# Unread columns left out in block two, the rotated keys' tile holds both weight parts, modulation chunks regrouped, square-root table loads moved, output in four pieces

## What is computed

```
# block one, two layers, both token streams
shift, scale, gate = split(silu(c) @ w_ada[l] + b_ada[l])        # modulation
h = rms(x, norm_w[l]) * (1 + scale) + shift
qa, ka, va, qb, kb, vb, cq, ckv, kpe, z = split(h @ w_in[l])     # kpe: 64 columns, rotated keys of the third head group
x = x + gate * (concat(attention a, b, c) * silu(z)) @ w_out[l]

# block two, 16 meta tokens ahead of the 256 latent ones
hn = rms_norm(h, norm_mix_g)
u, gb_in, gc_in, v_in, ga_lin, gbr_lin = split(hn @ w_in_2)
y_a = pool(u) @ pool_w      # group i: mean over the last 2, 4, 8 or 16 positions, minus the token itself
y_b = (gb_in * causal_conv3(gc_in * v_in)) @ conv_out_w
h = h + (sigmoid(ga) * y_a + sigmoid(gbr) * y_b) @ w_o
h = h + (silu(gate) * up) @ w_down                               # of rms_norm(h) @ w_gate_up
return rms_norm(h, norm_final_g)[:, 16:]                         # the 16 meta positions are dropped
```

## Time and profile before

| | |
|---|---|
| median of 3 runs | 3471.76 us (3467.4 to 3475.43) |
| the profiled execution's own time | 3463.28 us |
| its span, first to last instruction | 3462.0 us |
| PE busy | 3311.9 us, 96% of the span |
| DVE, ACT busy | 1650.5 us (48%), 1359.4 us (39%) |
| granted PE clock, mean | 0.982 of full speed |
| read from HBM | 550.07 MB |

### The profile page before, as it was taken

How to read it: one execution, slowest core, us unless ns; L and a number is a source line. 1 busy time by engine, 2 the same in 40 slices (tenths; PEclk the granted TensorE clock), 3 DMA queues, 4 the chain that set the end, 5 groups by cost and what they waited for, 6 DMA issues and landing times.

```text
span 3462.0 us, 52180 instructions
## 1 busy us (share of the span) xinstructions
PE 3311.9 (96%) x21982; PEld 2870.4 (83%) x21982; DVE 1650.5 (48%) x2678; ACT 1359.4 (39%) x2179; POOL 172.5 (5%) x252
## 2 busy tenths in 40 slices
PE   6799999988999989999799999999999999999998
PEld 1488888863458888887459999999999999999998
DVE  0422233374563363355575675555555645545444
ACT  1422232344442263333454443344444444444343
POOL 2000000001001101000101000000000000000000
PEclk9999999998999999999899999999999999999999
DMA  9533222226744254443436455555555555555554
GB/s 344 187 122 122 91 93 96 84 74 239 251 174 151 92 193 142 140 134 108 156 119 200 151 182 177 182 178 189 186 186 188 165 186 187 189 186 186 189 185 138
DMA packets 154314, 566.06 MB, mean 164 GB/s; under 512 B 17472, under 2 KB 19648, under 8 KB 152928
## 3 DMA queue, kind: packets, MB, share of 16 engines
q1 hardware_dynamic: 147648, 529.52, 45.7%
q0 software_dynamic: 6432, 33.20, 2.7%
HBM read 550.07 MB, written 12.58 MB: 163 GB/s over the span
## 4 chain that ended last, share of the span: by engine, by line
PE 88%; DMA 5%; DVE 3%; ACT 2%; issue 1%; POOL 0%; SPq 0%; DVEq 0%; ACTq 0%; POOLq 0%
PE ps L695 20%; PE ps L696 20%; PE ps L697 20%; PE ps L688 7%; PE ps L690 7%; PE ps L689 7%; DMA sb_raw<-in_stream 5%; PE ps L614 2%; PE ps L816 1%; PE ps L802 1%; PE ps L779 1%; PE ps L795 1%; PE ps L770 1%; DVE sb_wlo L1236 1%; PE ps L727 1%
## 5 line engine op out<-in xcount | busy, mean ns | idle before, releaser
L1236 DVE TENSOR_TENSOR sb_wlo<-sb_raw,sb_whi 128x1024 fp32r<-128x1024 f32 (+1 forms) x818 | 996.8, 1219 | 1355.0 <-ACT sb_whi L891 1354.5
L891 ACT ACTIVATE sb_whi<-sb_raw 128x1024 fp32r<-128x1024 f32 (+1 forms) x818 | 859.4, 1051 | 1141.9 <-PE ps L697 912.3
L695 PE MATMUL ps<-sb_hn_hi,sb_whi 128*128 128x256 f32 (+1 forms) x2944 | 832.3, 283 | 4.1 <-DVE sb_hn_lo L1301 4.1
L696 PE MATMUL ps<-sb_hn_lo,sb_whi 128*128 128x256 f32 (+1 forms) x2944 | 832.7, 283 | 0.0
L697 PE MATMUL ps<-sb_hn_hi,sb_wlo 128*128 128x256 f32 (+1 forms) x2944 | 831.4, 282 | 0.0
L695 PEld LDWEIGHTS ps<-sb_hn_hi,sb_whi 128*128 128x128 f32 x2944 | 556.2, 189 | 4.7 <-DVE sb_hn_lo L1301 4.5
L696 PEld LDWEIGHTS ps<-sb_hn_lo,sb_whi 128*128 128x128 f32 x2944 | 555.8, 189 | 0.0
L697 PEld LDWEIGHTS ps<-sb_hn_hi,sb_wlo 128*128 128x128 f32 x2944 | 555.7, 189 | 0.0
L690 PE MATMUL ps<-sb_whi,sb_lo 128*128 128x512 f32 (+1 forms) x968 | 374.3, 387 | 0.0
L695 PE MATMUL ps<-sb_hi,sb_whi 128*128 128x512 f32 (+1 forms) x1056 | 359.9, 341 | 14.8 <-DVE sb_lo L1284 14.8
L696 PE MATMUL ps<-sb_lo,sb_whi 128*128 128x512 f32 (+1 forms) x1056 | 357.7, 339 | 0.0
(11 more groups left out here) (259 smaller groups left out, 3959.3 us busy)
## 6 DMA issues: line engine op xcount, KB each, us to landing
sb_raw<-in_stream SPq DMA_DIRECT2D x992, 512.0 KB, 3.4
sb_raw<-in_stream SPq DMA_DIRECT2D x18, 384.0 KB, 3.1
sb_T<-in_x POOLq DMA_DIRECT2D x1, 4096.0 KB, 16.0
z_scratch<-sb_scr POOLq DMA_DIRECT2D x16, 256.0 KB, 2.5
sb_zb<-z_scratch POOLq DMA_DIRECT2D x16, 256.0 KB, 3.4
sb_bias<-in_bias POOLq DMA_DIRECT2D x4, 1024.0 KB, 10.1
x_scratch<-sb_T POOLq DMA_DIRECT2D x1, 4096.0 KB, 11.5
sb_T<-in_x POOLq DMA_DIRECT2D x2, 1536.0 KB, 7.5
```

The source lines that it names most:

```text
L695: PE.matmul(o, whi[:, s, w], xh, start=k == 0, stop=False)
L696: PE.matmul(o, whi[:, s, w], xl, start=False, stop=False)
L891: AC.activation(whi[:, s, 0:width], raw[:, r, 0:width], ACT.Copy).then_inc(*hi.up((g.id, c)))
L1236: VE.tensor_tensor(wlo[:, s, 0:width], raw[:, r, 0:width], whi[:, s, 0:width].bitcast(F32), ALU.subtract).then_inc(*lo.up((g.id, c)))
```

## The change

It has five parts.

1. In block two, `u`, `gc` and `v` are made only for the columns that are read later: the last 256 plus the window's length (258, 260, 264, 272) for `u`, the last 258 for `gc` and `v`. The token operand now starts at column 272 - n of its row. The pooling sums on DVE and the copies out of PSUM are narrowed alike.
2. For `kpe`, DVE writes the low part over the second 64 columns of `whi`, so that one stationary tile holds both parts. PE runs two products per inner tile in place of three, and the four transposes become four float32 products with a constant 128x64 matrix, "fold" (two unit matrices one above the other), which adds the halves.
3. `ADA_PACE` of layer 0 goes from 3, 3, 2, 0 chunks in four slots to 4, 2, 2, 0.
4. The four "sqrt_table" steps go from behind the last squares to the first chunk of the third of the four groups of `wout`, `wo` and `down`.
5. At the end DVE multiplies tile by tile with the norm's weight while `down` still runs, into a new tile `scaled`; when the norm is there, four multiplications of 1024 columns follow, and SP sends each piece (512 KB) by a transfer of its own.

```diff
--- before.py
+++ after.py
...
-ADA_PACE = ([8, 0] + [3, 3, 2, 0] * 11, [8, 0] + [2, 2, 2, 2, 0, 0] * 3)
+ADA_PACE = ([8, 0] + [4, 2, 2, 0] * 11, [8, 0] + [2, 2, 2, 2, 0, 0] * 3)
...
-    ("ident", P), ("band", 5 * P), ("cols", GRID_W), ("cos", 2 * HD), ("sin", 2 * HD), ("mean", 1), ("sum4", 2),
+    ("ident", P), ("fold", HD), ("band", 5 * P), ("cols", GRID_W), ("cos", 2 * HD), ("sin", 2 * HD), ("mean", 1), ("sum4", 2),
...
     for g in range(4):
-        mix.append(Group("u", None, g, DT, 512, span(512 * g), N2, "hn", 4, "w_in_2", "hn_mix" if g == 0 else None))
+        mix.append(Group("u", None, g, DT, 512, span(512 * g), L + WINDOWS[g], "hn", 4, "w_in_2", "hn_mix" if g == 0 else None))
     for j in range(4):
-        mix.append(Group("gc", None, j, DT, 512, span(2 * D + 512 * j), N2, "hn", 1, "w_in_2"))
+        mix.append(Group("gc", None, j, DT, 512, span(2 * D + 512 * j), L + 2, "hn", 1, "w_in_2"))
...
-        mix.append(Group("v", None, j, DT, 512, span(3 * D + 512 * j), N2, "hn", 1, "w_in_2"))
+        mix.append(Group("v", None, j, DT, 512, span(3 * D + 512 * j), L + 2, "hn", 1, "w_in_2"))
...
                 self.add("chunk", g, c)
+                if g.kind in ("wout", "wo", "down") and g.index == 2 and c == 0:
+                    self.add("sqrt_table")
...
         pl.flush()
-        pl.add("sqrt_table")
...
     pl.flush()
-    pl.add("sqrt_table")
...
     pl.flush()
-    pl.add("sqrt_table")
...
-    x_out, out_out = sig("x_out", 16), sig("out_out", 16)
+    x_out = sig("x_out", 16)
+    out_out = [sig(f"out_out{j}", 16) for j in range(4)]
...
+    SCALED = sb("scaled", [P, DT, L], F32, hn_at + 4 * N2 * 4)
...
         if g.x in ("hn", "latent"):
-            a = META if g.x == "latent" else 0
+            a = 0 if g.kind == "ffn" else N2 - g.n
             return NH[:, k, a:a + g.n], NL[:, k, a:a + g.n]
...
-        SP.wait_ge(*v_ev.at("final"))
-        SP.dma_start(d["out"], RES[:, :, META:]).then_inc(*out_out.up("out"))
-        SP.wait_ge(*out_out.at("out"))
+        for j in range(4):
+            SP.wait_ge(*v_ev.at("final", j))
+            SP.dma_start(d["out"][:, 4 * j:4 * j + 4, :], SCALED[:, 4 * j:4 * j + 4, :]).then_inc(*out_out[j].up("out"))
+        for j in range(4):
+            SP.wait_ge(*out_out[j].at("out"))
...
@@ -692,6 +695,10 @@
                     for t in range(g.width // P):
                         o = PS[:, g.base + t, 0:g.n]
                         w = slice(w0 + t * P, w0 + t * P + P)
+                        if g.kind == "kpe":
+                            PE.matmul(o, whi[:, s, w], xh, start=k == 0, stop=False)
+                            mm = PE.matmul(o, whi[:, s, w], xl, start=False, stop=k == g.kt - 1)
+                            continue
                         PE.matmul(o, whi[:, s, w], xh, start=k == 0, stop=False)
                         PE.matmul(o, whi[:, s, w], xl, start=False, stop=False)
                         mm = PE.matmul(o, wlo[:, s, w], xh, start=False, stop=k == g.kt - 1)
...
                     for t in range(4):
-                        mm = PE.transpose(PS[:, g.base, t * P:(t + 1) * P], SC[:, 7, t * P:(t + 1) * P], ident)
+                        mm = PE.matmul(PS[:, g.base, t * P:t * P + HD], SC[:, 7, t * P:(t + 1) * P], C("fold"), start=True,
+                                       stop=True)
                     mm.then_inc(*e_ev.up(("kpt", l)))
...
-                AC.activation(T2[:, 4 * (p % 2), 16:16 + N2], PS[:, g.base + p, 0:N2], ACT.Copy).then_inc(
+                AC.activation(T2[:, 4 * (p % 2), 16 + N2 - g.n:16 + N2], PS[:, g.base + p, 0:g.n], ACT.Copy).then_inc(
...
-                    ins = AC.activation(CV[:, m, 0:N2], PS[:, g.base + m, 0:N2], ACT.Copy)
+                    ins = AC.activation(CV[:, m, META - 2:N2], PS[:, g.base + m, 0:g.n], ACT.Copy)
...
+            if g.kind == "kpe":
+                v = whi[:, s, 0:width].rearrange("p (a b) -> p a b", b=P)[:, :, HD:P]
+                w_ = raw[:, r, 0:width].rearrange("p (a b) -> p a b", b=P)[:, :, HD:P]
+                VE.tensor_tensor(v, w_, v.bitcast(F32), ALU.subtract).then_inc(*lo.up((g.id, c)))
+                return
...
+        def scaled_out(k):
+            VE.tensor_scalar(SCALED[:, k, :], RES[:, k, META:], Pm("norm_final", k), None, ALU.mult).then_inc(*v_ev.up())
...
+                if g.kind == "down" and k < DT - 4:
+                    VE.wait_ge(*v_ev.last())
+                    scaled_out(k)
...
-                    VE.tensor_tensor(T2[:, dst, 16:16 + N2], T2[:, src, 16:16 + N2], T2[:, src, 16 - step:16 + N2 - step],
-                                     ALU.add).then_inc(*v_ev.up())
+                    a, b = 16 + N2 - g.n + 2 * step - 1, 16 + N2
+                    VE.tensor_tensor(T2[:, dst, a:b], T2[:, src, a:b], T2[:, src, a - step:b - step], ALU.add).then_inc(
+                        *v_ev.up())
...
-                    ins = VE.tensor_tensor(CV[:, m, 0:N2], CV[:, m, 0:N2], PS[:, g.base + m, 0:N2], ALU.mult)
+                    o = CV[:, m, META - 2:N2]
+                    ins = VE.tensor_tensor(o, o, PS[:, g.base + m, 0:g.n], ALU.mult)
...
             elif st[0] == "final":
+                VE.wait_ge(*v_ev.at("x", "down", DT - 1))
+                for k in range(DT - 4, DT):
+                    scaled_out(k)
+                VE.wait_ge(*v_ev.last())
                 rstd("down", T4[:, 1, :])
-                for k in range(DT):
-                    ins = VE.scalar_tensor_tensor(RES[:, k, META:], RES[:, k, META:], Pm("norm_final", k),
-                                                  T4[:, 1, 0:L], ALU.mult, ALU.mult)
-                ins.then_inc(*v_ev.up(("final",)))
+                for j in range(4):
+                    o = SCALED[:, 4 * j:4 * j + 4, :]
+                    VE.tensor_tensor(o, o, T4[:, 1, 0:L].unsqueeze(1).to_broadcast([P, 4, L]), ALU.mult).then_inc(
+                        *v_ev.up(("final", j)))
...
+    put("fold", np.tile(np.eye(HD, dtype=np.float32), (2, 1)))
```

## The result

The changed kernel takes 3442.2 us (median of 5 runs, 3440.5 to 3451.9) against 3473.8 beside it (3467.4 to 3476.0): a ratio of 0.9922 over all fast executions, 95% interval 0.9908 to 0.9936, or 27 us less (22 to 32); the two medians alone differ by 31.6. Forecast were 25.1 us less and 3446.7. The profiled executions are 3440.9 us against 3462.0, so 21.1 of it can be looked for in the two traces.

The account below looks back on a forecast made before the run. PE, busy 96% of the span, was taken as the bound. The terms 13.1 + 6.0 + 0 + 6.0 gave 25.1 us less, 3446.7 against a median of 3471.8; range 3440 to 3454, for 8 in 10 3437 to 3460.

Parts of the forecast that it names:

- Part 1: Narrower products of u, gc and v in block two: 28,032 fewer columns, all on PE's path, 13.1 us gained.
- I take 118.9: Pace assumed for products of 258 columns in block two, in ns, between estimates of 118.4 and 119.6.
- its sign of being wrong: The forecast is wrong if PE waits for DVE or ACT inside u, gc or v.
- The 0.49 read from 272 to 256: Block two: a column's worth in ns, from 7.8 ns over 16 columns; gave at most 13.7 us.
- Part 2: Rotated keys, kpe: 32 fewer products save 7.3 us, the folds give back 1.3; net 6.0 us gained.
- Part 3: Layer 0's modulation pace: same work ahead of chunk 4, so 0 us; ends 15 us gained or 2 lost.
- Rival (b): Layer 0's modulation waits vanish as the second slot asks for two chunks; 15 us more, 3431.7; chance 0.07.
- Part 4: Square root table loads moved into the stream: 0.7 us gained at the end of down, 0 at three other places.
- Part 5: Program's end: scaling ahead and output in four pieces, last landing at 3456.0; 6.0 us gained, table load included.
- (a): Pace of u, gc and v goes by 64-byte pieces, so narrowing gains nothing; sum 12.0 us, 3459.8; chance 0.10.
- (c): Starts off a 64-byte boundary slow PE's reads of hn_hi and hn_lo: 134.4 ns a product, 3478.8; chance 0.03.
- (d): Output pieces at the end don't overlap: 5.3 us less gain, 3452.0; chance included in the forecast's 0.77.

Follow-up runs that it names:

- e1: The changed kernel with layer 0's modulation pace set back from 4, 2, 2, 0 to 3, 3, 2, 0; 3446.5 us, 0.9937 of the kernel before.
- e9: The changed kernel with the columns read by the products of gc and v set group by group (start and width); one execution took 3438.9 us.
- e4: The kernel before with only the rotated-keys change (two kpe products in place of three, and the fold); 3462.9 us, 0.9982.
- e2: The kernel before with only layer 0's modulation pace changed to 4, 2, 2, 0; 3465.7 us against 3468.7, 0.9993.
- e10: The changed kernel with the four square root table loads back behind the last squares; 3447.2 us, 0.9926 of the kernel before.
- e5: The changed kernel once more, unchanged; 3442.3 us, 0.9920 of the kernel before.
- e8: The changed kernel with layer 0's modulation pace 2, 2, 2, 2 in place of 4, 2, 2, 0; 3417.1 us, 0.9855 of the kernel before.
- e11: The changed kernel with layer 0's modulation pace 3, 3, 1, 1; 3455.5 us, 0.9957 of the kernel before.
- e12: The changed kernel with layer 0's pace 2, 2, 2, 2 and both layers' first eight chunks as 4, 4; 3419.5 us, 0.9850 of the kernel before.
- e7: The changed kernel with the output in one 2 MB transfer in place of four of 512 KB; 3448.8 us, 0.9940 of the kernel before.

## Why the prediction was right, and where its steps were off

The sum was 25.1 us; the runs say 27, within an interval of some 5. The traces of the parts add up to 24.7 (11.1 + 6.3 + 0 + 7.3), and their own times to 22 (8.3 + 6.2 + 2.4 + 5.5 by the ratios, each within 3 to 4). That 24.7 stands so close to 25.1 is in part luck: part 1 was sized 2.0 too large and part 5 1.3 too small. It is made up like this:

**Part 1**, forecast 13.1, measured 11.1 (part 1 with an equal fall of the clock). The mechanism held: fewer columns, and nearly all of it on the path. The term was sized too large in "I take 118.9": 258 columns cost 119.5 (`v`, and `gc` between chunks 2 and 6), and a place of 14 columns gave 5.9 ns, not 6.5. (The 118.4 ahead of it should be 118.6 by its own numbers.) From PE's first product of `u` 0 to its first of `ga` 0 are 403.8 us before and 392.7 in e1, 11.1 less for 28,032 columns. 0.65 of what the columns gave went into the new waits in `gc` 1 to 3, against the prediction's "All of it is on the path" and its sign of being wrong. Without them the slope is 0.42 ns a column, one cycle at 2.4 GHz (0.417), so the other 1.3 of the missing 2.0 are the slope that was taken too steep. The 0.49 read from 272 to 256 was no slope, since e9 shows that 256 from 16 has a low price of its own. So the slope in the Trainium skill's rule ("TensorE: Matmul & The Clock Gate", Back-to-back issue gap, where it stands for the isolated gap of one product), which the prediction quoted and didn't take, was the better; these traces agree with it.

**Part 2**, forecast 6.0, measured 6.3 (3.17 + 3.15; e4 6.2 by the ratio). A fold costs 0.46 us more than the transposes, not 0.63 (0.98 - 0.35).

**Part 3**, forecast 0, measured 2.4 less, within 3 (e2), which can't be told from 0. The reason given was half right. "From chunk 0 to chunk 4 PE does the same work before and now" is wrong: four chunks together cost 1.86 us, and three and one 1.84 and 0.98, so PE comes to chunk 4 earlier. In group 13 it needs 4.55 us from chunk 0 to chunk 4 before and 3.58 after, without the wait. What holds the time is the load, issued when chunk 0 is done. PE's gain before chunk 4 becomes wait at chunk 4: over the eleven turns (groups 9 to 19), the idle time ahead of chunks 4 and 5 was 5.4 us before and 15.8 after (2.3 + 3.1, 11.0 + 4.8), and from chunk 0 to chunk 4 it stayed at 4.8 us a turn.

Rival (b) was rightly kept low for this change; with another pace the waits do go. Its bound of 15 us was too small then, because it counted one turn's 1.4 us of wait eleven times and no price of the odd chunks. The eleven turns of before take 68.8 us for the modulation products and their waits, and 51.5 without waits (3, 3 and 2 chunks at 1.84, 1.84 and 1.00): 17.3 lost, 3.0 of them in group 12. Pairs alone save another 0.68 a turn.

**Part 4**, forecast 0.7 at the end and nothing elsewhere, measured 0.7 at the end (e10). "I give the other three places 0" fails at `wo`: 0.5 us there (e10 against e1, e5, e8 and e11), and 0 only where the clock falls early, as in the profile of before. The prediction had looked at `wout` alone, where PE releases the root with the load and without it.

**Part 5, part 4's 0.7 in it**, forecast 6.0, measured 7.3. The step that failed is "limited by the bytes, 3448.5 + 7.5". The end is set by the last multiplication: the last piece is issued right behind it and lands 3.1 us later. Of the 7.3 are 0.7 the table, 1.8 the multiplications, 3.2 the pieces, 1.2 the packed source, and in some executions 0.5 that the products ahead of `L1271` ran before the clock fell (0.71 us in place of 1.22). Two of eight executions (e5, e12) did not have these 0.5, and their end took 81.9 and 81.4 us, not 80.6: there PE's mean was 0.8 slower as well, or the last square 0.3 later. The estimate from the Trainium skill's rule in the prediction, by which a piece lands some 3.2 us after its issue and the last one at 3455.1, came nearer than what I took: by the trace each piece took only 0.15 us longer than the one before it, 2.67 to 3.12.

**Rivals.** (a) is refuted: 272 and 258 columns touch the same 17 pieces of 64 bytes, and 258 is 5.9 ns cheaper. (c) is refuted: 258 from 14 cost 119.5, not 131. Yet a start has a price in one case, the 2.6 ns of e9. (d) is refuted by the changed kernel's own trace: from the first issue to the end are 6.6 us (3434.34 to 3440.9), where four pieces one behind another at 3.4 would take 13.6. (By the prediction's own numbers (d) costs 6.1, not 5.3.)

Not forecast: how much one execution's trace can differ in one stretch. The profile of before had the shortest attention of all and that of after one of the longest, which is most of why the difference of the two comes out some 6 us under that of the times (21.1 against 27).

## What to carry to other kernels

When a wait ends on a load whose buffer an earlier step gives back, count the work between giving back and needing again, in time and not in instructions: what is saved within that distance turns into wait, and only a longer distance helps. Products that fill only a part of the array should come in sets that fill it, and with their operands there together, since an odd one costs as much as the set. A difference of some us in one stretch of one trace is no effect until a kernel with that stretch unchanged has been seen without it.

## What the runs showed of the hardware beyond that

- 256 columns from column 16 at 117.0 ns, from column 14 at 119.6 (both in `gc`), and 264 from 0 and from 8 both at 121.9: the start matters for 256, by 1.1 ns the other way for 258, and not for 264. The same 256 columns cost 120.0 in block one, which I didn't try to explain.
- A product for 32 partitions runs beside others for the other 96. A chunk has two such products, and until the next full-width product one chunk takes 0.98 us, two 1.00, three 1.84, four 1.86.
- Four loads of 512 KB behind one another can land much later than 3.4 us. In e8, the loads of chunks 4 to 7 of group 8 landed 4.1, 7.6, 10.6 and 12.1 us after their issue.
- Writing 2 MB took 6.4 us from packed rows and 7.6 from 1 KB pieces, from the end of the last multiplication (e7, and before).
